# Rotary partners by VectorE's shuffle in place of products with a permutation matrix

## The chip, the cores and the metric

The kernel runs on one core of a Trainium2 chip. What counts is the device time of the whole kernel in microseconds (us), the median of several executions.

## What is computed

Two transformer blocks run one after the other over 512 tokens of width 1024, in fp32. The first mixes a gated recurrence over four heads with a windowed attention of eight query heads, then has a cross attention to a memory and a convolutional feed-forward part. The second runs a latent attention (MLA) and an attention to selected keys. Rotary embeddings stand in three places: on queries and keys of the windowed attention (the first 16 of 64 features of a head), and on the 32 rotary features of queries and of the one key of the latent attention.

```python
def rope(x, pos):
    half = x.shape[-1] // 2
    ...
    x1, x2 = x[..., :half], x[..., half:]
    return jnp.concatenate([x1 * cos - x2 * sin, x1 * sin + x2 * cos], axis=-1)
...
    qa = partial_rotary(q_a.reshape(B, S, ATT_Q_HEADS, ATT_HEAD_DIM), positions)
    ka = partial_rotary(k_a.reshape(B, S, ATT_KV_HEADS, ATT_HEAD_DIM), positions)
...
        q_nope, q_pe = q[..., :MLA_NOPE], rope(q[..., MLA_NOPE:], pos)
        k_pe = rope(k_rope[:, :, None, :], pos)[:, :, 0, :]
```

So each feature needs its partner, half a head away: x * cos + partner * sin, where the partner of the lower half carries a minus sign.

## The kernel before

Activations lie with features on the 128 partitions and the 512 tokens along the free axis. Every projection is three passes of TensorE (`three`, L579): weights and activations are split into a high and a low part. The weights come in slots of 128 x 1024 through a ring of four buffers; GpSimd splits each slot (`split`, L528: a tiny operation on `tick`, L533, then the high part, L534, then the low part, L536), two slots ahead at most, and starts on one when TensorE has finished the slot two before it.

All projections and transposes go through PSUM banks 0 and 1 in turn. `STREAM` (L80) lists them: an entry is a product with its number of slots, 0 where it takes no weights. Entry g uses bank g % 2, and `open_bank` (L574) waits until entry g - 2 has been read out (`freed`). The order of work on each engine is written out by hand, and engines meet only through semaphores.

A rotation took one product with a permutation matrix (`rotate` of TensorE, L640; the matrix `perm` swaps partners and carries the sign) into PSUM. VectorE then ran three operations (`rotate`, L1726): partners times sine (L1733), x times cosine in place (L1734), their sum (L1737). An fp32 product of 128x512 shows as two matmul records.

There are eight rotations. Those of the four query chunks `qa` and of the keys `ka` lie in the last head (h = 3) of the recurrence of the first block. TensorE runs products 0 and 1 in step `beside(3, 0)`, before `output(2)` (L781), and products 2 and 3 in `beside(3, 1)`, after the projection `k_a`; then come `tile_decays(3, 2)` (L733), `tile_scores(3, 1)` (L746), the projection `g_first`, `tile_decays(3, 3)`, and `tile_scores(3, 2)`, which needs `lev` of `select(3, 1)` (L1851). The keys' product stands between the transposes of `v_a` (L614) and the projection `g_rest`. VectorE rotates queries 0 and 1 before `tile(3, 1)` and queries 2 and 3 between `select(3, 0)` and `tile(3, 2)`; a `tile` is a run of 24 short products (L1842), a `select` one product with `level` (L1851) and one reduction (L1857). ScalarE makes the exponents of a tile (L1307). The keys are rotated after `select(3, 3)`. These five products had entries of their own in `STREAM`: `q_turn`, `q_turn2` and `k_turn`.

In the second block the key `kp` is rotated beside the gate `z_a`. The query chunks `qp` are rotated behind `ukv_k`: TensorE's two products stand before `ukv_v`, VectorE's part in the middle of the 16 rounds of `top_keys(1, r)` (L2239 to L2242). After that and two projections of `q_b` all three engines meet at a barrier (L555), before the latent attention.

Of the kernel before, what the change touches and what calls it, by code (L numbers as in the profile page):

```python
# [20 lines left out]
ALU = mybir.AluOpType  # L21
# [60 lines left out]
    ("q_turn", [0] * 2), ("k_a", [1]), ("q_turn2", [0] * 2), ("g_first", [1]), ("v_a", [1, 0]),  # L82
    ("k_turn", [0]), ("g_rest", [1] * 3),
# [25 lines left out]


def q_turn(c):

    return FIRST["q_turn"] + c if c < 2 else FIRST["q_turn2"] + c - 2
# [116 lines left out]
CONST_A = [("level", 8 * P), ("perm", P), ("band", 3 * P), ("spread", S), ("pick", P)]  # L230
CONST_D = [("perm", P), ("cos", S), ("sin", S), ("causal", S), ("onehot", TOEP), ("rep_k", P), ("rep_r", P), ("rep_p", P),
# [6 lines left out]
def build(nc, stream, xT, memT, pos, vecs, ident_d, const_r, const_a, const_d, sink_d, relb_d, gvec, x1_d, out_d):  # L238
    with ExitStack() as ctx:
# [185 lines left out]
        OUT_BANK = [(2, 3), (4, 5), (6, 1), (7, 0)]  # L425
# [51 lines left out]
        rot_done, rot_used, rotated = sem("rot_done"), sem("rot_used"), sem("rotated")  # L477
# [71 lines left out]
        def _(pe):  # L549
# [90 lines left out]
            def rotate(name, n, src, raw, perm, at=None, to=None):  # L640

                m = ROTATE[name] + n
                out_of_bank(pe, raw)
                if at is not None:
                    out = open_bank(at)
                else:
                    if n >= 2:
                        pe.wait_ge(rot_used, n - 1)
                    out = bank(4 + m % 2 if to is None else to)
                mm(out, perm, src, start=True, stop=True).then_inc(rot_done, 1)  # L650

# [35 lines left out]
            def recurrence(beside):  # L687
# [100 lines left out]
                for n in range(2):  # L788
                    pe.wait_ge(spreads, n + 1)
                    mm(bank(6 + n), c_a("pick", 0, P), wide[:, n, :], start=True, stop=True).then_inc(widened, 1)  # L790
# [151 lines left out]
            def head_beside(h, j):  # L942
                if h + 2 < HG_HEADS:
                    head_step(h + 2, j)
                elif h + 2 == HG_HEADS and j < 4:
                    project("q_a", j, 1, n_parts)
                elif h + 1 == HG_HEADS:
                    if j == 1:
                        project("k_a", 0, 1, n_parts)
                    if j < 2:  # L950
                        for c in (2 * j, 2 * j + 1):
                            rotate("first", c, qa[:, c, :], FIRST["q_a"] + c, c_a("perm", 0, P), q_turn(c))
                    elif j == 2:
                        project("v_a", 0, 1, n_parts)
                    elif j == 3:
                        turn_chunk("v_a", 0, 1, TURNED["v_a"])
                        rotate("first", 4, ka[:, :], FIRST["k_a"], c_a("perm", 0, P), FIRST["k_turn"])
                    elif j == 4:
                        project("g_rest", 0, 1, n_parts)
# [111 lines left out]
            rotate("second", 0, pk[:, :], FIRST["small"], c_d("rep_p", 0, P), to=6)  # L1071
# [36 lines left out]
            for c in range(2):  # L1108
                rotate("second", 1 + c, qp[:, c, :], FIRST["uq"] + 4 + c, c_d("perm", 0, P))

# [55 lines left out]
            def token_squares(x, start, stop):  # L1166
                for i in range(ST):
                    last = mm(bank(0)[:, i:i + 1], x[:, P * i:P * i + P], ones[:, 0:1],
                              start=start and i == 0, stop=stop and i == ST - 1)
                return last  # L1170
# [23 lines left out]
        def _(act):  # L1194
# [444 lines left out]
            A(ycol[:, :], bank(0)[:, :ST], ACT.Sqrt, scale=1.0 / D, bias=EPS).then_inc(std_made, 1)  # L1639
# [7 lines left out]
        def _(dve):  # L1647
# [78 lines left out]
            def rotate(name, n, x, cos, sin, at=None, to=None):  # L1726
                m = ROTATE[name] + n
                dve.wait_ge(rot_done, m + 1)
                if m:
                    dve.wait_ge(rotated, m)  # L1730
                partners, read = (bank(4 + m % 2 if to is None else to), rot_used) if at is None else (bank(at % 2), freed[at % 2])
                part = (sq if name == "second" else sgb)[:, m % 2, :]
                V.tensor_tensor(part, partners, sin, ALU.mult).then_inc(read, 1)  # L1733
                own(V.tensor_tensor(x, x, cos, ALU.mult))  # L1734
                if at is not None:
                    out_of_bank(dve, at)
                V.tensor_tensor(x, x, part, ALU.add).then_inc(rotated, 1)  # L1737
# [32 lines left out]
            def recurrence():  # L1770
# [117 lines left out]
                def turn_queries(c):  # L1888
                    rotate("first", c, qa[:, c, :], cosA[:, :], sinA[:, :], q_turn(c))

                for h in range(HG_HEADS):
                    more = h + 1 < HG_HEADS
                    if not more:
                        dve.wait_ge(tables, 2)
                        for c in (0, 1):
                            out_of_bank(dve, FIRST[f"head{2 + c}"] + 2)
                            turn_queries(c)
                    tile(h, 1)
                    select(h, 0)
                    if more:  # L1900
                        forget(h + 1)
                    else:
                        turn_queries(2)
                        turn_queries(3)
                    tile(h, 2)
                    select(h, 1)
                    tile(h, 3)
                    select(h, 2)
                    if more:
                        logs_low(h + 1)  # L1910
                    if h + 2 < HG_HEADS:
                        queries(h + 2)
                    select(h, 3)
                    if more:
                        start(h + 1)
                    else:
                        rotate("first", 4, ka[:, :], cosA[:, :], sinA[:, :], FIRST["k_turn"])
# [311 lines left out]
            rotate("second", 0, kp[:, :], c_d("cos", 0, S), c_d("sin", 0, S), to=6)  # L2229
# [47 lines left out]
            for c in range(2):  # L2277
                rotate("second", 1 + c, qp[:, c, :], c_d("cos", 0, S), c_d("sin", 0, S))
# [83 lines left out]
def rotary_partners(group, half):  # L2362

    m = np.zeros((P, P), np.float32)
    for g in range(0, P, group):
        for r in range(half):
            m[g + half + r, g + r] = -1.0
            m[g + r, g + half + r] = 1.0
    return m


def constants_a():
    c = level_constants()
    c["perm"] = rotary_partners(64, ROT_HALF)
# [6 lines left out]
    for g in (0, 64):  # L2381
        for r in range(2 * ROT_HALF):
            c["pick"][P // ROT_HALF * (r % ROT_HALF):P // ROT_HALF * (r % ROT_HALF + 1), g + r] = 1.0
    return [np.concatenate([np.asarray(c[n], np.float32) for n, _ in table], 1) for table in (CONST_R, CONST_A)]


def constants_d():
    c = {"perm": rotary_partners(32, 16)}
    freqs = np.float32(10000.0) ** (-np.arange(16, dtype=np.float32) / np.float32(16))
    angle = np.arange(S, dtype=np.float32)[None, :] * freqs[np.arange(P) % 16][:, None]  # L2390
    c["cos"], c["sin"] = np.cos(angle), np.sin(angle)
# [13 lines left out]
    c["rep_p"] = np.roll(c["perm"] * (np.arange(P)[:, None] < 32), 32, 0)[:, np.arange(P) % 32]  # L2405
# [123 lines left out]
```

## Time and profile before

| | |
|---|---|
| median of 3 runs | 1509.24 us (1509.18 to 1510.2) |
| the profiled execution | 1509.78 us, its span 1507.3 us |
| TensorE busy | 1449.6 us, 96% |
| VectorE busy | 942.1 us, 63% |
| GpSimd busy | 830.0 us, 55% |
| ScalarE busy | 453.8 us, 30% |
| TensorE in the chain that ended last | 81% |
| VectorE in that chain | 10% |

All times in the views are us from the start of the span. PE is TensorE, PEld its weight loads, PEldq its queue, DVE VectorE, ACT ScalarE, POOL GpSimd. A line of the chain tells what the end waited for at that moment; "issue" is time in which the engine waited for nothing that the profile shows. An idle time in brackets stands before the operation, with what ended it. `pair` is PSUM: two banks each. The granted clock (PEclk) is the share of full speed that TensorE was given: 1.00 is 2.4 GHz, 0.50 is 1.2 GHz.

### The profile page before, as it was taken

The page shows a single profiled execution, that of the slowest core. Times are in us where ns is not written, and L with a number is a line of the kernel's source. Part 1 is how long each engine was busy: PE and PEld are TensorE (multiplying, and loading weights), DVE is VectorE, ACT ScalarE, POOL GpSimd, SP SyncE. Part 2 cuts the span into 40 slices and gives each one's busy share as a digit, 9 for nine tenths or more (in the row PEclk, how much of TensorE's full clock was granted, in tenths as well). Part 3 has the DMA queues.
Part 4 walks back from the last instruction along what each step waited for, and adds up shares of the span by engine and source line. Part 5 has one row for each costly group of instructions (what it writes and reads, how often), then busy time and mean ns, then how long its engine had stood idle before and what let it go on. Part 6 is the DMA issues. An engine that isn't in the chain of part 4 may idle for free.

```text
span 1507.3 us, 19926 instructions
## 1 busy us (share of the span) xinstructions
PE 1449.6 (96%) x6948; PEld 1138.7 (76%) x6948; DVE 942.1 (63%) x1879; ACT 453.8 (30%) x887; POOL 830.0 (55%) x675
## 2 busy tenths in 40 slices
PE   4999999999999999999999999999999999999998
PEld 3777777676788788687888888887767777666887
DVE  6557797687238431567777764234767897686146
ACT  4555442366223111321010101112233334364112
POOL 3533323433566777266777777776655443444663
PEclk9999999999999999999999999999999999999999
DMA  5221111121333333132333333334225531322331
GB/s 205 72 70 43 43 42 43 56 66 54 106 97 98 112 112 103 51 98 84 98 98 98 98 97 99 98 112 134 84 73 153 105 89 46 113 78 88 117 96 67
DMA packets 37017, 135.59 MB, mean 90 GB/s; under 512 B 4296, under 2 KB 4552, under 8 KB 36296
## 3 DMA queue, kind: packets, MB, share of 16 engines
q1 hardware_dynamic: 33264, 121.13, 26.6%
q10 hardware_dynamic: 3672, 13.35, 3.4%
q8 instruction: 55, 0.90, 0.3%
q14 instruction: 26, 0.21, 0.0%
HBM read 127.64 MB, written 6.82 MB: 89 GB/s over the span
## 4 chain that ended last, share of the span: by engine, by line
PE 81%; DVE 10%; issue 4%; ACT 2%; POOL 1%; PEld 1%; DMA 0%; PEldq 0%; ACTq 0%; DVEq 0%; POOLq 0%
PE pair L581 23%; PE pair L583 22%; PE pair L582 22%; PE pair L851 3%; PE pair L879 3%; DVE X L1842 2%; PE pair L863 2%; PE pair L781 1%; DVE sums L1686 1%; POOL wL L536 1%; DVE lev L1851 1%; DVE rstd L1698 1%; DVE dx L1996 1%; POOL wH L534 1%; ACT E L1307 0%
## 5 line engine op out<-in xcount | busy, mean ns | idle before, releaser
L536 POOL TENSOR_TENSOR wL<-ring,wH 128x1024 fp32r<-128x1024 f32 x223 | 546.0, 2448 | 18.6
L581 PE MATMUL pair<-nH,wH 128*128 128x512 f32 x1064 | 426.9, 401 | 13.3 <-DVE nL L1677 8.2
L583 PE MATMUL pair<-nH,wL 128*128 128x512 f32 x1064 | 415.8, 391 | 0.0
L582 PE MATMUL pair<-nL,wH 128*128 128x512 f32 x1064 | 415.7, 391 | 0.0
L533 POOL TENSOR_TENSOR tick<-tick 128x1 f32<-128x1 f32 x223 | 55.5, 249 | 640.4 <-PE pair L583 631.1
L581 PEld LDWEIGHTS pair<-nH,wH 128*128 128x128 f32 x1064 | 200.1, 188 | 78.3 <-issue 27.5
L534 POOL TENSOR_SCALAR wH<-ring 128x1024 fp32r<-128x1024 f32 x223 | 237.4, 1065 | 0.0
L583 PEld LDWEIGHTS pair<-nH,wL 128*128 128x128 f32 x1064 | 200.3, 188 | 43.0
L582 PEld LDWEIGHTS pair<-nL,wH 128*128 128x128 f32 x1064 | 200.5, 188 | 40.4 <-issue 1.4
L1523 ACT ACTIVATE sgb<-cv 128x512 f32<-128x512 f32 x22 | 13.9, 634 | 209.6 <-DVE cv L2162 209.6
L1686 DVE TENSOR_TENSOR sums<-sums,sq 128x512 f32<-128x512 f32 (+1 forms) x37 | 60.1, 1623 | 18.4 <-ACT sq L1227 17.1
L581 PE MATMUL pair<-aH,wH 128*128 128x512 f32 x176 | 69.1, 393 | 0.0
L583 PE MATMUL pair<-aH,wL 128*128 128x512 f32 x176 | 68.6, 390 | 0.0
L582 PE MATMUL pair<-aL,wH 128*128 128x512 f32 x176 | 68.5, 389 | 0.0
L1842 DVE TENSOR_TENSOR X<-E,qT 128x64 f32<-128x64 f32 x192 | 35.1, 223 | 43.0 <-ACT E L1307 43.0
L2161 DVE SCALAR_TENSOR_TENSOR cv<-gpad,vec,cv 128x512 f32<-128x512 f32 x22 | 56.7, 2578 | 0.8
L1380 ACT ACTIVATE dx<-dx,stat 128x128 f32<-128x128 f32 (+3 forms) x64 | 36.0, 562 | 63.2 <-DVE stat L2002 63.0
L2188 DVE TENSOR_TENSOR hT<-pair,hT 128x512 f32<-128x512 f32 x8 | 5.5, 692 | 78.5 <-PE pair L583 78.5
L2014 DVE TENSOR_SCALAR dx<-dx,stat 128x128 f32<-128x128 f32 (+3 forms) x64 | 52.2, 816 | 2.3
L2158 DVE TENSOR_TENSOR gpad<-pair,rstd 128x512 f32<-128x512 f32 x22 | 15.2, 692 | 55.8 <-PE pair L583 55.8
L1307 ACT ACTIVATE E<-pair 128x768 f32<-128x768 f32 (+1 forms) x40 | 32.0, 852 | 42.4 <-PE pair L692 24.9
L1227 ACT ACTIVATE sq<-hT 128x512 f32<-128x512 f32 x28 | 17.7, 631 | 81.3 <-DVE hT L1743 48.3
(387 smaller groups left out, 2644.0 us busy)
## 6 DMA issues: line engine op xcount, KB each, us to landing
ring<-stream SPq DMA_DIRECT2D x223, 512.0 KB, 3.6
gvec<-gv ACTq DMA_DIRECT2D x1, 2560.0 KB
hT<-xT SPq DMA_DIRECT2D x4, 512.0 KB, 5.6
x_d<-hT ACTq DMA_DIRECT2D x1, 2048.0 KB, 7.2
toep<-gvec ACTq DMA_DIRECT2D x8, 256.0 KB, 3.5
hT<-x_d ACTq DMA_DIRECT2D x1, 2048.0 KB, 9.2
out<-yo SPq DMA_DIRECT2D x4, 512.0 KB, 3.6
cD<-const_d ACTq DMA_DIRECT2D x1, 1345.0 KB, 6.4
```

Source lines behind the costliest of these rows:

```text
L533: pool.tensor_tensor(tick[:, 1:2], tick[:, 0:1], tick[:, 0:1], ALU.add).then_inc(high_done, 1)
L534: pool.tensor_scalar(wH[:, r % SPL, :], ring[:, r, :], 1.0, 0.0, ALU.mult, ALU.add).then_inc(high_done, 1)
L536: pool.tensor_tensor(wL[:, r % SPL, :], ring[:, r, :], wH[:, r % SPL, :].bitcast(F32), ALU.subtract).then_inc(split_done, 1)
L581: mm(out, a[0], b[0], start=first, stop=False)
L582: mm(out, a[0], b[1], start=False, stop=False)
L583: return mm(out, a[1], b[0], start=False, stop=last)
L851: last = mm(out, *pairs[t], start=t == 0, stop=t == count - 1)
L879: last = mm(out[rows, qs], w, turned[:, j % 2, t, qs], start=n_t == 0, stop=n_t == len(kind["serves"]) - 1)
L1686: V.tensor_tensor(sums[:, :width], sums[:, :width], sq[:, a % 2, :width], ALU.add).then_inc(sq_added, 1)
L1842: last = V.tensor_tensor(two(X[:, m % 2, kind, xs])[:, half], factor(kind, d), two(src)[:, half], ALU.mult)
L2014: V.tensor_scalar(px, px, st[:, 5:6], None, ALU.mult).then_inc(a_prob, 1)
L2161: own(V.scalar_tensor_tensor(out=y, in0=x[:, 0:S], scalar=w[0], in1=y, op0=ALU.mult, op1=ALU.add))
```

## The change

Partners no longer come from TensorE. VectorE's `stream_shuffle` permutes partitions within each group of 32: it writes the partners of x to an SBUF buffer, and the product with the sine is then made in place in that buffer. The minus sign moves into the sine tables: the table of the first block is spread with `signed` in place of `pick`, and that of the second is made with its sign. The five entries without weights leave `STREAM`, so that everything after them changes between bank 0 and bank 1; the last products of the kernel follow with `last_bank`. The constants `perm` (twice) and `rep_p` go.

```diff
 STREAM = [
     ("head0", HEAD), ("head1", HEAD), ("head2", HEAD), ("head3", HEAD), ("q_a", [1] * 4),
-    ("q_turn", [0] * 2), ("k_a", [1]), ("q_turn2", [0] * 2), ("g_first", [1]), ("v_a", [1, 0]),
-    ("k_turn", [0]), ("g_rest", [1] * 3),
+    ("k_a", [1]), ("g_first", [1]), ("v_a", [1, 0]), ("g_rest", [1] * 3),
...
-CONST_A = [("level", 8 * P), ("perm", P), ("band", 3 * P), ("spread", S), ("pick", P)]
-CONST_D = [("perm", P), ("cos", S), ("sin", S), ("causal", S), ("onehot", TOEP), ("rep_k", P), ("rep_r", P), ("rep_p", P),
+CONST_A = [("level", 8 * P), ("signed", P), ("band", 3 * P), ("spread", S), ("pick", P)]
+CONST_D = [("cos", S), ("sin", S), ("causal", S), ("onehot", TOEP), ("rep_k", P), ("rep_r", P),
...
-        OUT_BANK = [(2, 3), (4, 5), (6, 1), (7, 0)]
+        last_bank = (FIRST["out2"] + DC - 1) % 2
+        OUT_BANK = [(2, 3), (4, 5), (6, last_bank), (7, 1 - last_bank)]
...
-            def rotate(name, n, src, raw, perm, at=None, to=None):
-
-                m = ROTATE[name] + n
-                out_of_bank(pe, raw)
-                if at is not None:
-                    out = open_bank(at)
-                else:
-                    if n >= 2:
-                        pe.wait_ge(rot_used, n - 1)
-                    out = bank(4 + m % 2 if to is None else to)
-                mm(out, perm, src, start=True, stop=True).then_inc(rot_done, 1)
...
-                    mm(bank(6 + n), c_a("pick", 0, P), wide[:, n, :], start=True, stop=True).then_inc(widened, 1)
+                    mm(bank(6 + n), c_a(("signed", "pick")[n], 0, P), wide[:, n, :], start=True, stop=True).then_inc(widened, 1)
...
-                    if j < 2:
-                        for c in (2 * j, 2 * j + 1):
-                            rotate("first", c, qa[:, c, :], FIRST["q_a"] + c, c_a("perm", 0, P), q_turn(c))
...
-                        rotate("first", 4, ka[:, :], FIRST["k_a"], c_a("perm", 0, P), FIRST["k_turn"])
...
-            rotate("second", 0, pk[:, :], FIRST["small"], c_d("rep_p", 0, P), to=6)
...
-            for c in range(2):
-                rotate("second", 1 + c, qp[:, c, :], FIRST["uq"] + 4 + c, c_d("perm", 0, P))
-
...
-            def rotate(name, n, x, cos, sin, at=None, to=None):
+            def rotate(name, n, x, cos, sin, half, group):
+
+
                 m = ROTATE[name] + n
-                dve.wait_ge(rot_done, m + 1)
+                swap = [i + half if i % group < half else i - half if i % group < 2 * half else i for i in range(32)]
                 if m:
                     dve.wait_ge(rotated, m)
-                partners, read = (bank(4 + m % 2 if to is None else to), rot_used) if at is None else (bank(at % 2), freed[at % 2])
                 part = (sq if name == "second" else sgb)[:, m % 2, :]
-                V.tensor_tensor(part, partners, sin, ALU.mult).then_inc(read, 1)
+                V.stream_shuffle(part, x, swap).then_inc(swapped, 1)
+                dve.wait_ge(swapped, m + 1)
+                V.tensor_tensor(part, part, sin, ALU.mult).then_inc(part_made, 1)
                 own(V.tensor_tensor(x, x, cos, ALU.mult))
-                if at is not None:
-                    out_of_bank(dve, at)
+                dve.wait_ge(part_made, m + 1)
                 V.tensor_tensor(x, x, part, ALU.add).then_inc(rotated, 1)
...
                 def turn_queries(c):
-                    rotate("first", c, qa[:, c, :], cosA[:, :], sinA[:, :], q_turn(c))
+                    out_of_bank(dve, FIRST["q_a"] + c)
+                    rotate("first", c, qa[:, c, :], cosA[:, :], sinA[:, :], ROT_HALF, 32)
...
-                        rotate("first", 4, ka[:, :], cosA[:, :], sinA[:, :], FIRST["k_turn"])
+                        out_of_bank(dve, FIRST["k_a"])
+                        rotate("first", 4, ka[:, :], cosA[:, :], sinA[:, :], ROT_HALF, 32)
...
-            rotate("second", 0, kp[:, :], c_d("cos", 0, S), c_d("sin", 0, S), to=6)
+            rotate("second", 0, kp[:, :], c_d("cos", 0, S), c_d("sin", 0, S), 16, 32)
...
-                rotate("second", 1 + c, qp[:, c, :], c_d("cos", 0, S), c_d("sin", 0, S))
+                out_of_bank(dve, FIRST["uq"] + 4 + c)
+                rotate("second", 1 + c, qp[:, c, :], c_d("cos", 0, S), c_d("sin", 0, S), 16, 32)
...
+    c["signed"] = c["pick"] * np.where(np.arange(P) % 64 < ROT_HALF, -1.0, 1.0)
...
-    c["cos"], c["sin"] = np.cos(angle), np.sin(angle)
+    c["cos"] = np.cos(angle)
+    c["sin"] = np.sin(angle) * np.where(np.arange(P) % 32 < 16, -1.0, 1.0)[:, None]
```

## Rows read from the trace of the kernel before

**Rows 1.** The page: busy time by engine, and the shares of the chain that ended last
```profile
PE 1449.6 (96%) x6948; PEld 1138.7 (76%) x6948; DVE 942.1 (63%) x1879; ACT 453.8 (30%) x887; POOL 830.0 (55%) x675
...
PE 81%; DVE 10%; issue 4%; ACT 2%; POOL 1%; PEld 1%; DMA 0%; PEldq 0%; ACTq 0%; DVEq 0%; POOLq 0%
```

**Rows 2.** The chain in order of time, first block: start us, us, what
```profile
215.23 3.09 PE pair L650 x4
218.32 3.43 PE pair L781 x8
...
240.03 1.76 DVE X L1842 x13
...
244.64 1.58 PE pair L746 x12
...
255.34 0.86 PE pair L650 x2
...
264.33 5.25 PE pair L781 x8
```

**Rows 3.** Timeline of TensorE: start us, us, engine line op out<-in, count [idle before <-releaser]
```profile
213.83 0.45 PE L733 MATMUL pair<-cR,lftH 64*128 64x384 f32 x2 [2.03 <-ACT E L1307]
...
1142.09 1.88 PE L650 MATMUL pair<-qp,cD 128*128 128x512 f32 x4
```

**Rows 4.** Three stretches: us, busy by engine, granted clock (PEclk), DMA share, GB/s
```profile
215.00:218.30 3.30, 3.30 (x7) 1.50 (x6) 3.30 (x14) 1.51 (x2) 0.00 (x0) 0.61 0.00 0
264.30:269.70 5.40, 5.27 (x9) 1.89 (x8) 3.16 (x13) 0.28 (x2) 1.24 (x1) 0.68 0.32 97
1097.00:1104.00 7.00, 7.00 (x29) 4.78 (x26) 3.56 (x6) 1.96 (x5) 1.34 (x1) 1.00 0.25 75
```

**Rows 5.** Timeline of ScalarE, first block
```profile
215.28 1.51 ACT L1307 ACTIVATE E<-pair 128x768 f32<-128x768 f32 x2 [1.01 <-PE pair L733]
```

**Rows 6.** Timeline of VectorE, first block
```profile
169.70 2.96 DVE L1811 TENSOR_TENSOR E<-E,kk 128x256 f32<-128x256 f32 x2
...
228.79 0.36 DVE L1842 TENSOR_TENSOR X<-E,qT 128x64 f32<-128x64 f32 x2 [3.86 <-ACT E L1307]
...
235.77 1.49 DVE L1734 TENSOR_TENSOR qa<-qa,cosA 128x512 f32<-128x512 f32 x1
```

**Rows 7.** Timeline of VectorE: the operations nearest to a shuffle
```profile
216.79 0.29 DVE L1794 COPY xk<-kk 128x256 f32<-128x256 f32 x1
...
233.30 1.96 DVE L1857 TENSOR_REDUCE Sg<-lev 128x128 f32<-128x1024 f32 x1
```

**Rows 8.** Timeline of GpSimd, first block
```profile
169.32 2.72 POOL L536 TENSOR_TENSOR wL<-ring,wH 128x1024 fp32r<-128x1024 f32 x1
174.55 2.48 POOL L533 TENSOR_TENSOR tick<-tick 128x1 f32<-128x1 f32 x1 [2.51 <-PE pair L583]
...
234.34 2.38 POOL L536 TENSOR_TENSOR wL<-ring,wH 128x1024 fp32r<-128x1024 f32 x1
243.28 0.19 POOL L533 TENSOR_TENSOR tick<-tick 128x1 f32<-128x1 f32 x1 [6.56 <-PE pair L583]
```

**Rows 9.** The chain in order of time, second block
```profile
1094.61 1.99 issue
...
1098.95 0.86 PE pair L650 x2
...
1156.29 4.11 PEldq L555
```

**Rows 10.** Timeline of VectorE, second block
```profile
1105.96 0.69 DVE L1721 TENSOR_TENSOR za<-pair,sgb 128x512 f32<-128x512 f32 x1 [3.02 <-ACT sgb L1272]
...
1149.41 0.42 DVE L2239 MAX8 best<-selm 128x8 f32<-128x256 f32 x1
...
1155.30 1.09 DVE L2242 TENSOR_SCALAR selm<-selm 128x256 f32<-128x256 f32 x1
```

**Rows 11.** Timeline of GpSimd, second block
```profile
1149.70 1.05 POOL L534 TENSOR_SCALAR wH<-ring 128x1024 fp32r<-128x1024 f32 x1
```

More of the change, by code:

```diff
@@ L108, in running @@
     return at, n
-def q_turn(c):
-    return FIRST["q_turn"] + c if c < 2 else FIRST["q_turn2"] + c - 2
 def g_r(c):
@@ L476, in build @@
         y_left, y_right = sem("y_left"), sem("y_right")
-        rot_done, rot_used, rotated = sem("rot_done"), sem("rot_used"), sem("rotated")
+        swapped, part_made, rotated = sem("swapped"), sem("part_made"), sem("rotated")
         f_made, lf_made, lf_turned, lh_made, lft_made, zero_one = (
@@ L1167, in token_squares @@
                 for i in range(ST):
-                    last = mm(bank(0)[:, i:i + 1], x[:, P * i:P * i + P], ones[:, 0:1],
+                    last = mm(bank(1 - last_bank)[:, i:i + 1], x[:, P * i:P * i + P], ones[:, 0:1],
                               start=start and i == 0, stop=stop and i == ST - 1)
@@ L1638, in _ @@
             act.wait_ge(sum_done, NORMS.index("out") + 1)
-            A(ycol[:, :], bank(0)[:, :ST], ACT.Sqrt, scale=1.0 / D, bias=EPS).then_inc(std_made, 1)
+            A(ycol[:, :], bank(1 - last_bank)[:, :ST], ACT.Sqrt, scale=1.0 / D, bias=EPS).then_inc(std_made, 1)
             act.wait_ge(r_made, NORMS.index("out") + 1)
@@ L2359, in level_constants @@
     return out
[L2362 to L2369, printed above, removed]
 def constants_a():
     c = level_constants()
-    c["perm"] = rotary_partners(64, ROT_HALF)
     q, k = np.arange(P)[:, None], np.arange(3 * P)[None, :] - P
@@ L2383, in constants_a @@
             c["pick"][P // ROT_HALF * (r % ROT_HALF):P // ROT_HALF * (r % ROT_HALF + 1), g + r] = 1.0
+    c["signed"] = c["pick"] * np.where(np.arange(P) % 64 < ROT_HALF, -1.0, 1.0)
     return [np.concatenate([np.asarray(c[n], np.float32) for n, _ in table], 1) for table in (CONST_R, CONST_A)]
 def constants_d():
-    c = {"perm": rotary_partners(32, 16)}
+    c = {}
     freqs = np.float32(10000.0) ** (-np.arange(16, dtype=np.float32) / np.float32(16))
     angle = np.arange(S, dtype=np.float32)[None, :] * freqs[np.arange(P) % 16][:, None]
-    c["cos"], c["sin"] = np.cos(angle), np.sin(angle)
+    c["cos"] = np.cos(angle)
+    c["sin"] = np.sin(angle) * np.where(np.arange(P) % 32 < 16, -1.0, 1.0)[:, None]
     q, k = np.arange(P)[:, None], np.arange(S)[None, :] - (S - P)
@@ L2404, in constants_d @@
     c["rep_r"] = np.arange(P)[:, None] == 32 + np.arange(P)[None, :] % 32
-    c["rep_p"] = np.roll(c["perm"] * (np.arange(P)[:, None] < 32), 32, 0)[:, np.arange(P) % 32]
     c["parity"] = np.arange(P)[:, None] // 32 % 2 == np.arange(2)[None, :]
```

## The prediction

> **What bounds the kernel now.** I read the page's busy times first, then the shares of the chain that ended last. TensorE is busy 96% of the span and holds 81% of the chain; VectorE is busy 63% and holds 10% of it [rows 1]. So a product taken from TensorE is worth its length only where TensorE holds the chain, and a VectorE instruction added costs nothing only where it does not. The next view is therefore the chain in order of time around the eight products removed. Four fp32 products with `perm` stand for the queries of the first block, one for its keys, three for the second block; one product is two matmul records and takes 0.86 us on the chain, as the one at 255.34 [rows 2]. Around the first four the chain passes from TensorE to VectorE and back [rows 2]; that is where the argument is hard. Third come the timelines of VectorE, ScalarE and GpSimd there, and the granted clock.
>
> **First block, queries 0 and 1.** Their products hold the chain for 3.09 us, four records at 215.23 [rows 2], against 1.88 us for four such records at 1142.09, and TensorE had stood idle 2.03 us before L733 at 213.83 [rows 3]: the granted clock was 0.61 from 215.00 to 218.30, a mix of 1.2 and 2.4 GHz [rows 4]. With them gone, `output` (L781) still waits for ScalarE's exponents, which end at 215.28 + 1.51 = 216.79 [rows 5]. It starts 1.5 us earlier than 218.32 [rows 2], but runs its first microsecond in the slow clock; I take 1.0 us earlier (1.5 if the clock is back at once; 0.8 us later than now if the slow clock also covers all of L781, which cost 5.25 - 3.43 = 1.8 us once [rows 2]). After its two rotations VectorE idles 3.86 us before the run of products at 228.79 [rows 6]. Two shuffles fit in there.
>
> **What a shuffle costs.** The trace has none. The nearest rows are a copy of 256 elements at 0.29 us, so 0.6 for 512, and a reduction of 1024 elements at 1.96 us, so 1.0 for 512 [rows 7]. Nearest is the copy, which likewise has one input and one output; I take 0.7 with the wait behind it, and keep 0.6 and 1.0 as ends. The Trainium skill, "VectorE: DVE Perf Modes", section "The perf-mode tier table", gives a shuffle about 2400 ns for 2048 elements; scaled, an estimate of 0.6, which would make each pair of shuffles 0.2 us cheaper. No run here shows it.
>
> **Queries 2 and 3** lie between `select(3,0)` and `tile(3,2)`, where VectorE holds the chain from 228.79 to 244.64 [rows 2, 6]. Two shuffles add 1.4 us. A second effect comes with them: the product with the sine read PSUM and SBUF and now reads SBUF twice. In this trace VectorE products with two SBUF inputs wait while GpSimd splits weights: L1811 needed 2.96 us for a pair while the split ran 169.32 + 2.72 = 172.04 [rows 6, 8]. The cosine product at 235.77 took 1.49 us because the split at 234.34 ended at 236.72 [rows 6, 8]. After the change the sine product meets that wait instead, so it is not paid twice; the shuffle, with one input, runs beside the split, and that recovers about 0.1. Net: 1.0 earlier, 1.4 more, 0.1 back: TensorE gets `lev` at 244.95 in place of 244.64, 0.3 later (between 0.5 earlier and 2.2 later by the ends above).
>
> **The hole this leaves on TensorE.** Its part of the same stage loses another two products (1.9 us) and so finishes `g_first` at about 243.28 - 1.0 - 1.9 = 240.4, which is where GpSimd's next split would start (L533, now at 243.28) [rows 8]. With 0.9 us of decays behind it TensorE then idles from 241.3 to 244.95, 3.6 us; now it works through nearly all of this. The clock fell once after an idle stretch of 2.03 us, and again with L781 after narrow products (0.68 granted from 264.30 to 269.70) [rows 4]. I expect one more stretch at 1.2 GHz, right where TensorE takes over the chain. The price of a full one is the 1.8 us above; part of it may fall into the hole: 1.4 (ends 0 and 1.8).
>
> **Keys.** Product at 255.34, 0.86 us, TensorE before and after it on the chain [rows 2]: 0.86 gained. VectorE's shuffle is hidden there: nothing of the chain returns to VectorE before L781. First block: +0.3 + 1.4 - 0.86 = +0.8 us.
>
> **Second block, key.** 0.86 us at 1098.95, TensorE on the chain on both sides [rows 9]: gained. VectorE idles 3.02 us before the next gate at 1105.96 [rows 10], which hides 0.7.
>
> **Second block, queries.** Four records at 1142.09, two products, 1.72 us at 0.86 each [rows 3]. The next meeting of all engines is the barrier, which TensorE releases last, at 1156.29 + 4.11 = 1160.40 [rows 9]. Without these and the key's product it gets there at 1160.40 - 2.58 = 1157.82. VectorE is done at 1155.30 + 1.09 = 1156.39 [rows 10]. For it: 0.86 earlier, two shuffles 1.4 later, and the split. The split now at 1149.70 (L534, and L536 for another 2.4) moves 2.58 forward to 1147.1 and ends about 1150.7 [rows 8, 11]. Today the rotations are over at 1149.41 [rows 10] and miss it; then it lies across the whole second rotation, one of whose SBUF products waits up to 2.4 us. VectorE would end at 1156.39 - 0.86 + 1.4 + 2.4 = 1159.3, or 0.8 sooner if L2242 no longer meets a split. I take 1159.0: VectorE becomes the last at the barrier and 1.2 us of the gain is lost (ends 0 and 1.7, and 0.6 more for a shuffle of 1.0). Second block: -0.86 - 1.72 + 1.2 = -1.4 us.
>
> **At nothing:** the sign moved into tables (same copies and products as before, one constant for another of equal size), a 131 KB smaller constant load, the waits of `k_a` and `g_first` on older banks, and the swap of banks 0 and 1 for all that follows, since five entries leave the list; both banks are used alike. What hides the older waits is TensorE's own work on the entries between; without it they would cost less than a product.
>
> **Sum.** +0.8 - 1.4 = -0.6 us (0.55 unrounded). The profiled execution took 1509.78 with a span of 1507.3, 0.54 above the median of 1509.24. Against its own time the sum gives 1509.2; against the median 1508.7, my forecast. About 0.2%, 3.0 us, is what a measurement of this kernel can tell from no change.
>
> **Rivals.**
> Everything is covered (22%): the clock stays at 2.4 GHz behind the hole, the barrier stays TensorE's. Then 0.3 - 0.86 - 0.86 - 1.72 = -3.1, with the early gain at 1.5 in full -3.6; time 1505.8 in the middle. For it: after 1.99 us of idle time at 1094.61 the granted clock stayed at 1.00 [rows 4, 9]. Against: the hole is nearly twice that.
> The split meets the run of 24 short products (18%), slower than before. VectorE would begin `tile(3,2)` at 240.03 + 0.3 = 240.35 [rows 2], GpSimd its split at 240.4, together within the error of both. If GpSimd's L534 is in first, the run is held for 1.05 + 2.4 us, 3.2 of it lost, and TensorE waits: -0.6 + 3.2 = +2.6, 1511.9. It decides from a start of the run later than about 240.55 (a shuffle over 0.8, or an earlier split). Against it: at 174.55 GpSimd asked inside such a run and waited 2.48 us, to the run's end [rows 8]. The Trainium skill, "SBUF — State Buffer", section "Who interferes with whom", says the engine that issues first gets the shared ports for the whole instruction and the other blocks. By that rule the split would get in between two short products, which is this rival; the row at 174.55 shows it kept out of the run, and the rule agrees with the 2.96 us.
> The shuffle is dear, or takes part in the quarrel with GpSimd (10%): at 1.0 us each, 0.6 more in each place where VectorE decides, +0.6 in all: 1509.9.
> Forecast as worked out: 50%.
>
> **How the numbers follow.** Faster by over 0.2% needs the first rival, three parts in four of it, and little of the forecast: 0.20. Slower by over 0.2% needs the second, somewhat over half of it, and tails of the third and the forecast: 0.14. The rest, 0.66. The range runs from about the first rival's middle, 1505.6, to near the second's, 1511.6, which leaves half of each out, about one in five.
>
> **What would show it.** In the profile after: L781 near 217.3; VectorE's shuffles 0.6 to 0.7; a sine product stretched at about 235; TensorE idle over 3 us before the `lev` that it takes at about 244.9, with a granted clock under 1 behind; GpSimd's L533 at about 240.4 lasting 2 us or more (forecast) or VectorE's X products stretched (second rival); 0.86 less at the keys; at the barrier TensorE waiting for VectorE rather than the other way. The forecast is wrong if the clock stays up in the hole, if the barrier is still TensorE's, or if the split holds the run.

## The result, and the profile after

The changed kernel takes 1517.08 us (1515.12 to 1519.82), the kernel before beside it 1509.18 (1506.80 to 1510.20): a ratio of 1.0051, 95% interval 1.0039 to 1.0062, so slower by some 8 us. The forecast was 1508.7 with a range to 1511.6. The profiled execution took 1519.82 us with a span of 1517.8, 10.5 more than the span of before; all shifts in this section are between these two traces.

The page first: span, busy times and shares of the chain. Line numbers have moved: L764 is `output` (L781 before), L729 the scores over X (L746), L1709 to L1714 the rotation (L1733 to L1737), L1819 the run X (L1842), L1828 `lev` (L1851), L576 to L578 the split products (L581 to L583), L528, L529 and L531 GpSimd's tick, `wH` and `wL` (L533, L534, L536).

```profile
span 1517.8 us, 19905 instructions
PE 1449.2 (95%) x6932; PEld 1141.3 (75%) x6932; DVE 953.8 (63%) x1895; ACT 454.1 (30%) x887; POOL 829.7 (55%) x675
PE 81%; DVE 11%; issue 3%; ACT 2%; POOL 1%; DMA 0%; ACTq 0%; DVEq 0%; POOLq 0%
```

Sixteen matmul records are gone, and yet TensorE is as long busy as before (1449.6 in [rows 1]): what remains ran longer. VectorE has 11.7 us more. Next, the chain in order of time in the first block: start us, us, what.

```profile
215.61 1.52 ACT E L1282 x2
217.27 5.19 PE pair L764 x8
...
235.92 0.76 DVE sgb L1709 x2
236.70 1.24 DVE sgb L1711
...
242.10 4.80 DVE X L1819 x13
246.90 1.57 DVE X L1819 x11
248.47 1.15 DVE lev L1828
249.75 2.90 PE pair L729 x12
```

`output` starts 1.05 us earlier than at 218.32 [rows 2], as forecast, but takes 5.19 us in place of 3.43. The run X of tile 2, 3.3 us before (1.76 and 1.57 in that trace's chain), takes 6.37. Why, the timelines of GpSimd and VectorE show:

```profile
242.06 0.19 POOL L528 TENSOR_TENSOR tick<-tick 128x1 f32<-128x1 f32 x1 [4.67 <-PE pair L578]
242.21 1.04 POOL L529 TENSOR_SCALAR wH<-ring 128x1024 fp32r<-128x1024 f32 x1
243.34 2.34 POOL L531 TENSOR_TENSOR wL<-ring,wH 128x1024 fp32r<-128x1024 f32 x1
```

```profile
241.49 0.69 DVE L1714 TENSOR_TENSOR qa<-qa,sgb 128x512 f32<-128x512 f32 x1
242.10 1.23 DVE L1819 TENSOR_TENSOR X<-E,qT 128x64 f32<-128x64 f32 x2
243.25 2.51 DVE L1819 TENSOR_TENSOR X<-E,kk 128x64 f32<-128x64 f32 x2
245.69 0.35 DVE L1819 TENSOR_TENSOR X<-E,qT 128x64 f32<-128x64 f32 x2
```

Two of these short products need 0.35 us. The first pair ends with GpSimd's `wH` (243.25), the second with its `wL` (245.68), and only then does the run go on. This is the mechanism of the prediction's second rival; its price of 3.2 us measured 3.0.

TensorE's side, with the idle time before each, and the granted clock of the stretches behind (us, busy by engine, PEclk, DMA share, GB/s). 0.50 is the lower of the two levels, 1.2 GHz, throughout.

```profile
249.75 2.90 PE L729 MATMUL pair<-X 128*128 128x128 f32 x12 [6.95 <-DVE lev L1828]
1168.36 0.49 PE L834 MATMUL pair<-kn,qn 64*128 64x128 f32 x4 [1.60 <-DVEq L1628]
```

```profile
217.27:222.46 5.19, 5.19 (x10) 2.41 (x11) 5.16 (x30) 0.00 (x0) 0.00 (x0) 0.71 0.00 0
249.75:254.50 4.75, 4.75 (x19) 4.54 (x20) 4.75 (x24) 0.00 (x0) 0.00 (x0) 0.50 0.00 0
1170.32:1176.00 5.68, 5.68 (x13) 4.45 (x14) 2.86 (x10) 2.59 (x6) 0.22 (x1) 0.50 0.62 97
```

The second block's end on VectorE and GpSimd:

```profile
1156.29 0.74 DVE L1709 STREAM_SHUFFLE sq<-qp 128x512 f32<-128x512 f32 x1
1157.07 0.70 DVE L1711 TENSOR_TENSOR sq<-sq,cD 128x512 f32<-128x512 f32 x1
1157.69 2.88 DVE L1712 TENSOR_TENSOR qp<-qp,cD 128x512 f32<-128x512 f32 x1
1160.60 0.69 DVE L1714 TENSOR_TENSOR qp<-qp,sq 128x512 f32<-128x512 f32 x1
...
1167.11 1.14 DVE L2221 TENSOR_SCALAR selm<-selm 128x256 f32<-128x256 f32 x1
```

```profile
1157.31 2.71 POOL L531 TENSOR_TENSOR wL<-ring,wH 128x1024 fp32r<-128x1024 f32 x1
...
1166.90 0.19 POOL L528 TENSOR_TENSOR tick<-tick 128x1 f32<-128x1 f32 x1 [1.76 <-PE pair L578]
1167.06 1.04 POOL L529 TENSOR_SCALAR wH<-ring 128x1024 fp32r<-128x1024 f32 x1
```

The cosine product, 0.68 us alone, waits for `wL`; the last instruction ahead of the barrier meets `wH` (it took 1.09 in [rows 10] too, but there 4 us before TensorE arrived). TensorE stands 1.60 us.

Laying the same instructions of both traces beside each other gives this account, in us of delay against before, each entry the growth of the shift from one instruction to the next:

| Where | Adds | Shift then |
|---|---|---|
| `output` and what leads to it, slow clock | +0.70 | 0.70 |
| rotations of queries 2 and 3: started 0.05 later, 6.18 in place of 4.86 | +1.37 | 2.07 |
| run X of tile 2 held by the split | +3.03 | 5.10 |
| slow clock behind TensorE's 6.9 us without work | +2.25 | 7.34 |
| the keys' product gone | -0.94 | 6.40 |
| drift to 1080 us | +0.15 | 6.55 |
| a sums product of 1081.8 held by `wH`, where before it came first; slow clock behind | +0.90, +1.61 | 9.06 |
| second block's key product gone | -0.86 | 8.20 |
| its queries' two products gone | -1.76 | 6.44 |
| VectorE late at the barrier | +1.48 | 7.92 |
| slow clock behind the barrier | +2.68 | 10.60 |

The profiled execution lies 2.7 us above the median. That is about one entry of clock, and the likeliest reading is that not every execution has all of them; this is argued, since only one execution has a trace.

### The profile page after: what moved, and what is told of

Read it like the earlier page. It is cut to its first block, busy times and chain, and to the rows that moved or that the text cites. A ratio compares the mean times of both kernels' runs of the same rounds, so it can differ in the third digit from the quotient of the medians.

```text
span 1517.8 us, 19905 instructions
## 1 busy us (share of the span) xinstructions
PE 1449.2 (95%) x6932; PEld 1141.3 (75%) x6932; DVE 953.8 (63%) x1895; ACT 454.1 (30%) x887; POOL 829.7 (55%) x675
## 4 chain that ended last, share of the span: by engine, by line
PE 81%; DVE 11%; issue 3%; ACT 2%; POOL 1%; DMA 0%; ACTq 0%; DVEq 0%; POOLq 0%
PE pair L576 23%; PE pair L578 22%; PE pair L577 22%; PE pair L834 3%; PE pair L862 3%; DVE X L1819 2%; PE pair L846 2%; PE pair L764 1%; DVE sums L1661 1%; POOL wL L531 1%; DVE lev L1828 1%; DVE rstd L1673 1%; DVE dx L1975 1%; DVE selm L2232 1%; ACT E L1282 1%
## 5 line engine op out<-in xcount | busy, mean ns | idle before, releaser
L531 POOL TENSOR_TENSOR wL<-ring,wH 128x1024 fp32r<-128x1024 f32 x223 | 545.9, 2448 | 18.6
L576 PE MATMUL pair<-nH,wH 128*128 128x512 f32 x1064 | 429.3, 403 | 13.4 <-DVE nL L1652 8.2
L578 PE MATMUL pair<-nH,wL 128*128 128x512 f32 x1064 | 417.2, 392 | 0.0
L528 POOL TENSOR_TENSOR tick<-tick 128x1 f32<-128x1 f32 x223 | 55.7, 250 | 651.3 <-PE pair L578 641.9
L576 PEld LDWEIGHTS pair<-nH,wH 128*128 128x128 f32 x1064 | 201.3, 189 | 78.2 <-issue 27.5
L529 POOL TENSOR_SCALAR wH<-ring 128x1024 fp32r<-128x1024 f32 x223 | 236.8, 1062 | 0.0
L578 PEld LDWEIGHTS pair<-nH,wL 128*128 128x128 f32 x1064 | 201.2, 189 | 43.3
L576 PE MATMUL pair<-aH,wH 128*128 128x512 f32 x176 | 69.0, 392 | 0.0
L578 PE MATMUL pair<-aH,wL 128*128 128x512 f32 x176 | 68.5, 389 | 0.0
L1819 DVE TENSOR_TENSOR X<-E,qT 128x64 f32<-128x64 f32 x192 | 36.0, 230 | 42.1 <-ACT E L1282 42.1
```

The lines of the kernel that those rows point to most:

```text
L528: pool.tensor_tensor(tick[:, 1:2], tick[:, 0:1], tick[:, 0:1], ALU.add).then_inc(high_done, 1)
L529: pool.tensor_scalar(wH[:, r % SPL, :], ring[:, r, :], 1.0, 0.0, ALU.mult, ALU.add).then_inc(high_done, 1)
L531: pool.tensor_tensor(wL[:, r % SPL, :], ring[:, r, :], wH[:, r % SPL, :].bitcast(F32), ALU.subtract).then_inc(split_done, 1)
L576: mm(out, a[0], b[0], start=first, stop=False)
L578: return mm(out, a[1], b[0], start=False, stop=last)
L1819: last = V.tensor_tensor(two(X[:, m % 2, kind, xs])[:, half], factor(kind, d), two(src)[:, half], ALU.mult)
```

## Experiments

They go from "which half" to "which wait" to "which order of work avoids it". In each, "before" is the kernel before, run beside it: 1509.45 us for `one_moved` and the three `early3` kernels, 1509.4 for `first_moved` and the two `spaced` ones, 1509.36 for the other eight.

### One block at a time

In `first_only` the second block keeps its three products, in `second_only` the first keeps its five. The edits are the change's own hunks, for one block only.

> First block by shuffle, second block by products as in the kernel before. The theory: the loss arises in the first block, where VectorE's rotations of queries 2 and 3 end so late that GpSimd's split gets in ahead of tile 2's short products X (3.0 us of stall) and TensorE, idle for some 7 us, gets the slow clock afterwards. It expects about 1516 us (1514.5 to 1517.5), X run of tile 2 at 242 us with rows of 1.2 and 2.5 us in it, and the end of the first block some 6 us late. Rival: the loss is spread over both blocks, 1512 us.

> First block by products as before, second block by shuffle. The theory: three products less on TensorE (-2.6 us), VectorE late at the barrier by 1.5 us, and perhaps one stretch of slow clock behind that wait (up to 2.7 us): 1508.0 to 1510.8, most likely 1509.5. Rival (the second block carries a half of the loss): 1513 us.

Measured: `first_only` 1517.08, ratio 1.0053 (1.0039 to 1.0067); `second_only` 1508.37, ratio 0.9997 (0.9988 to 1.0006). The whole loss is the first block's. Its trace repeats the one above: TensorE idle 6.95 us before tile 2's `lev`. The second block's trace has TensorE waiting 1.60 us at the barrier, and no gain that can be measured.

### The products kept for nothing

`first_filled`: VectorE shuffles in the first block, and TensorE still makes the five products (with another matrix of the same size), which nobody reads.

```
 # VectorE, first block (condensed)
+own(V.stream_shuffle(part, x, swap)); partners = part
 V.tensor_tensor(part, partners, sin, ALU.mult).then_inc(read, 1)   # read frees the product's bank
```

> The kernel before, but in the first block VectorE takes the partners from its shuffle, and TensorE still makes its five products, which nobody reads; second block as before. The theory (VectorE is late, whatever TensorE does in the meantime): the X run of tile 2 is still met by the split if it starts at 242 us, and the time is 1513 to 1516. Rival (the hole on TensorE, which the products filled, costs the time through the clock): the products fill it, and the time is 1509 to 1511.

Measured: 1513.42, ratio 1.0026 (1.0016 to 1.0037), 3.7 us below `first_only` with the same work on VectorE. The number is the theory's, its reason is not. VectorE (first fence) and GpSimd (second):

```profile
243.13 0.35 DVE L1845 TENSOR_TENSOR X<-E,qT 128x64 f32<-128x64 f32 x2
...
246.38 1.22 DVE L1854 TENSOR_TENSOR lev<-pair,cA 128x1024 f32<-128x1024 f32 x1
```

```profile
244.95 1.57 POOL L533 TENSOR_TENSOR tick<-tick 128x1 f32<-128x1 f32 x1 [6.54 <-PE pair L583]
```

The run starts 1 us later than in the changed kernel and isn't held: the split is released by TensorE's last product out of that slot of weights, and the rotary products ahead of it on TensorE put that off to 244.95, into the run, where the tick waits for the run's end. So the products removed had paced the split: with them it asks 1.8 us after the run's start, without them 0.04 us before it. The same rotations with a split released at 242.06 (changed kernel) or 242.67 (`first_only`) cost 3 us more. What is left, 4.1 us by the medians, shows in this trace as the longer pair of rotations (1.4) and as slow clock ahead of them (1.6) and behind TensorE's 2.06 us without work (1.6).

### Shorter rotations, and products gone alone

Both leave the partners out, and with them the shuffle, `no_shuffle23` for queries 2 and 3, `no_shuffle_all` for all eight. The sine product reads x itself:

```
-V.stream_shuffle(part, x, swap)
-V.tensor_tensor(part, part, sin, ALU.mult)
+V.tensor_tensor(part, x, sin, ALU.mult)
```

> The kernel after without the shuffle in the rotations of queries 2 and 3 (the partners are left out there: the sine product reads the query itself), so that each is one instruction of 0.75 us shorter. The theory (a race at 242.1 us between GpSimd's split and tile 2's X run, lost by 0.04 us): the run now starts at 240.6, before the split's tick at 242.1, which has to wait for its end; the run takes 3.3 us in place of 6.4, TensorE's idle stretch falls from 6.9 to about 2.4 us, and the time is that of after less 1.5, less 3.0, less up to 1.4 of clock: 1511.0 to 1513.0. Rival (the time follows the length of VectorE's work alone): 1517.1 - 1.5 = 1515.6.

> The kernel after with all eight shuffles left out (the partners are left out: the sine product reads the row block itself): VectorE does as much as in the kernel before, TensorE has eight products less. It prices the removal of the products alone. Theory: X run before the split as above, second block 2.6 us shorter on TensorE and VectorE late at the barrier by no more than 0.3: 1508 to 1510.5. Rival (holes on TensorE without its products cost the time by the clock): 1513 or more.

Measured: 1513.99, ratio 1.0026 (1.0017 to 1.0035), and 1514.11, ratio 1.0027 (1.0016 to 1.0037). VectorE and GpSimd in `no_shuffle23`:

```profile
236.33 2.03 DVE L1710 TENSOR_TENSOR sgb<-qa,sinA 128x512 f32<-128x512 f32 x1
...
241.73 0.36 DVE L1822 TENSOR_TENSOR X<-E,qT 128x64 f32<-128x64 f32 x2
```

```profile
242.49 2.62 POOL L528 TENSOR_TENSOR tick<-tick 128x1 f32<-128x1 f32 x1 [4.68 <-PE pair L578]
```

The race is shown: a run that starts 0.76 us ahead of the tick keeps GpSimd out to its end, 2.62 us; TensorE's idle stretch is 3.09 us in place of 6.95. But the two shuffles left out (1.5 us) shortened the pair of rotations by only 0.78: the sine product then stands in the split itself. 3.1 us came back, less than expected, and one part of that miss is this. The other shows in `no_shuffle_all`, where I missed by 3.6 us and the rival's number held. In its profiled execution the shift against before is -0.3 us at 264 and +0.1 at the barrier, so neither block loses by work; it comes behind the barrier, 2.8 us of it, in a stretch of slow clock after TensorE's 1.60 us. Taking TensorE's products away, with VectorE no slower than before, makes holes of 1.70, 3.09 and 1.60 us. In this execution the clock fell behind the first and the last of them and stayed at 1.00 behind the second. The execution, 1512.22, lies 1.9 us below the median, and no trace shows what the others had besides.

### The rotations put elsewhere

`moved` turns query 2 ahead of tile 1's run (VectorE idled 2.89 us there) and query 3 after the selection of tile 2 (3.36 us). `one_moved` moves only query 3. `first_moved` is `moved` with the second block's products kept.

```
 # last head, condensed
 for c in (0, 1): ... turn_queries(c)
+turn_queries(2)                  # moved, first_moved
 tile(h, 1); select(h, 0)
-turn_queries(2); turn_queries(3) # one_moved keeps query 2 here
 tile(h, 2); select(h, 1); tile(h, 3); select(h, 2)
+turn_queries(3)
 ...
```

> The kernel after, with query 2's rotation put ahead of tile 1's X run, where VectorE idles 2.9 us, and query 3's behind tile 3's X run and the selection of tile 2, where it idles 3.4 us. The theory (late rotations and the split in the X run): tile 2's X run starts at about 236 us without a stall, TensorE's idle stretch of 6.9 us goes to below 1 us, and the time is 1508.0 to 1510.5. Rival (removing TensorE's work makes the holes, wherever VectorE puts its own): 1513 to 1516.

> The kernel after with query 3's rotation alone put behind tile 3's X run and the selection of tile 2; query 2's stays where it was. The theory (a race for the ports at 242 us): tile 2's X run starts at about 239.5 and is nearly over when the split comes, so that one rotation of some 3.5 us put off saves more than its own length: tile 2's lev at 243 us in place of 248.4, and the time is 1509.5 to 1511.5. Rival (each rotation costs its own length, both the same): halfway between after and the kernel with both moved, 1513.5.

> First block by shuffle with query 2's rotation ahead of tile 1 and query 3's behind tile 3's X run and the selection of tile 2, second block by products as before. The theory: the first block ends 1.8 to 2.0 us earlier than before, as in the trace of 'moved', the second is that of the kernel before: 1507.0 to 1508.5. Rival (the 2 us in that trace were a matter of where the slow clock fell): 1509.0 to 1510.0.

Measured: `moved` 1509.87, ratio 1.0001 (0.9992 to 1.0011); `one_moved` 1510.07, ratio 1.0003 (0.9991 to 1.0015); `first_moved` 1509.55, ratio 0.9999 (0.9990 to 1.0008). The order alone gives back the 7 us. In `one_moved` VectorE reads

```profile
239.57 0.36 DVE L1819 TENSOR_TENSOR X<-E,qT 128x64 f32<-128x64 f32 x2
...
242.82 1.22 DVE L1828 TENSOR_TENSOR lev<-pair,cA 128x1024 f32<-128x1024 f32 x1
```

The second row is 5.6 us before the 248.38 of the changed kernel, for one rotation of some 3.5 us taken from the path: the run was 2.9 us old when the split's tick came at 242.47. The median falls as far as with both moved. That is a race decided, not a length: the rival's 1513.5 is out.

`first_moved` missed, and the rival's number held. Its trace is 1.6 us ahead of before at 264 and 0.3 behind at 1100: behind the 1.99 us without work that TensorE has at 1095 in both kernels, the clock falls in this one and did not in the profile of before. That is not a trait of this kernel: of the fifteen traces with this wait twelve fell to 0.68 behind it, `before_early3` (products in both blocks) among them, and three stayed at 1.00, those of before, of the changed kernel and of `second_only`. In `moved` that stretch reads (second row; the first is behind the barrier)

```profile
1159.14:1164.00 4.86, 3.62 (x21) 2.91 (x22) 3.60 (x15) 3.25 (x7) 2.17 (x1) 1.00 0.51 81
1094.73:1100.00 5.27, 5.27 (x15) 3.20 (x16) 1.20 (x3) 2.46 (x5) 1.72 (x1) 0.68 0.36 99
```

### The barrier of the second block

`moved`, `one_moved`, `second_only` and `no_shuffle_all` all wait 1.60 us there, though VectorE's load differs. First I took VectorE's length for the cause and shifted work. In the `early` kernels the final norm's products go ahead of the second reciprocal (all eight, or three in `early3`), and rounds of the top-keys search take their place:

```
 # condensed
 norm("q_lat", ...)
+for c in range(3): final_normed(c)        # range(8) in the first form
 inverse("c_kv")
```

> The kernel before, with the eight products of the final norm on VectorE put ahead of the reciprocal of the second block, where VectorE idles some 5 us, and three rounds of the top-keys search taken forward into the places they leave. Control for the next run: VectorE isn't late at the barrier there, so nothing changes: 1509.2, 1508.3 to 1510.0. Rival (this shift is worth something by itself): below 1507.5.

> The kernel 'moved' with the same shift in the second block. The theory: TensorE's wait of 1.60 us for VectorE at the barrier goes, and with it the slow clock that some runs have behind it: 1505.5 to 1508.3, most likely 1507.0. Rival (another releaser is as late at the barrier, or the wait costs nothing): 1509.0 to 1510.

> The kernel 'moved' with three of the final norm's products (2.1 us) put where VectorE idles 3.7 us before the second reciprocal, clear of the split that comes 1 us later, and two rounds of top keys taken forward into their place. The theory: VectorE's last instruction before the barrier starts before the split's tick and isn't stretched from 0.29 to 1.14 us, TensorE's wait of 1.60 us at the barrier falls to below 0.7, the slow clock behind it goes, and the time is 1505.5 to 1508.0. Rival (the three products meet the split as the eight did, and put off the second reciprocal): above 1510, with the wait ahead of the transposes of the new keys above 2.5 us in place of 1.99.

> The kernel 'second_only' (first block by products, second by shuffle) with the same shift of three products. The theory: -2.6 us for the products without the wait at the barrier: 1506.0 to 1507.5. Rival as above: above 1509.

> The kernel before with the same shift of three products, as a control: VectorE is 3.8 us early at the barrier there, so both theories that blame VectorE's lateness expect nothing: 1509.2 (1508.5 to 1510.0). Rival: the shift is worth something or costs something by itself, over 1.5 us either way.

Measured: `before_early` 1515.47, ratio 1.0038 (1.0024 to 1.0052; the profiled execution was its fastest, 1511.50), `moved_early` 1513.34, ratio 1.0020 (1.0010 to 1.0030). VectorE and TensorE in the first:

```profile
1083.26 8.31 DVE L2225 SCALAR_TENSOR_TENSOR hT<-hT,vec,rstd 128x512 f32<-128x512 f32 x8
```

```profile
1097.74 1.09 PE L1067 MATMUL pair<-ident,pk 128*128 128x128 f32 x4 [6.47 <-issue]
```

Eight products of 5.5 us took 8.31, since a split lay across them; the reciprocal came after them, and TensorE passed on 4.5 us later than with its usual 1.99. So "issue" in front of those transposes is a wait for VectorE's `c_kv` in all the kernels, and the idle time ahead of the reciprocal was no cover for 5.5 us. With three of them: `moved_early3` 1509.73, ratio 1.0000 (0.9991 to 1.0008), `second_early3` 1509.94, 1.0001 (0.9992 to 1.0011), `before_early3` 1509.95, 1.0000 (0.9991 to 1.0008). They do no harm, and no good: the wait is 1.60 us as ever. It is the split's length and not VectorE's: in the changed kernel TensorE stops at 1166.76, the tick starts at 1166.90, VectorE's last instruction 0.2 us later, `wH` ends at 1168.10 and that instruction with it. VectorE in `moved_early3`:

```profile
1143.71 2.92 DVE L1711 TENSOR_TENSOR sq<-sq,cD 128x512 f32<-128x512 f32 x1
...
1149.49 2.88 DVE L1712 TENSOR_TENSOR qp<-qp,cD 128x512 f32<-128x512 f32 x1
...
1158.91 1.14 DVE L2224 TENSOR_SCALAR selm<-selm 128x256 f32<-128x256 f32 x1
```

The 2 us saved ahead of the rotations were handed to the split: the first sine product, 0.95 in `moved`, now takes 2.92. The splits come at TensorE's pace, and VectorE's products with two SBUF inputs fall in step with them. The remedy is then not less work but another order. `moved_spaced` and `second_spaced` put the second rotation four rounds of top keys later, where no split runs; those rounds (MAX8, MATCH_REPLACE8) are not stretched by splits in these traces.

```
 for c in range(2):
     rotate("second", 1 + c, qp[:, c, :], ...)
-for r in range(10, 16): top_keys(1, r)
+    for r in ((10, 11, 12, 13), (14, 15))[c]: top_keys(1, r)
```

> The kernel 'moved' with four rounds of top keys put between the two rotations of the second block's queries, so that the second rotation starts some 4 us later and its four instructions run between two splits. The theory: its cosine product takes 0.7 us and not 2.9, VectorE reaches its last instruction 2.2 us earlier, before the split's tick, which takes that one from 1.14 to 0.29 us; TensorE's 1.60 us at the barrier falls to below 0.7, and the time is 1506.0 to 1508.5. Rival (the hold only moves to another product, as with 'moved_early3'): the wait stays 1.60 and the time 1509.0 to 1510.5.

> The kernel 'second_only' with the same order of rounds and rotations. The theory: 1506.0 to 1508.0, the wait at the barrier below 0.7. Rival: wait of 1.60 us and 1508.0 to 1509.5.

Measured: `moved_spaced` 1506.47 (1504.72 to 1507.42), ratio 0.9979 (0.9970 to 0.9988); `second_spaced` 1506.86, ratio 0.9985 (0.9976 to 0.9994). VectorE, then TensorE and GpSimd, in `moved_spaced`:

```profile
1152.55 0.69 DVE L1711 TENSOR_TENSOR sq<-sq,cD 128x512 f32<-128x512 f32 x1
1153.15 0.69 DVE L1712 TENSOR_TENSOR qp<-qp,cD 128x512 f32<-128x512 f32 x1
1153.88 1.57 DVE L1714 TENSOR_TENSOR qp<-qp,sq 128x512 f32<-128x512 f32 x1
...
1157.32 0.53 DVE L2221 TENSOR_SCALAR selm<-selm 128x256 f32<-128x256 f32 x1
```

```profile
1158.65 0.49 PE L834 MATMUL pair<-kn,qn 64*128 64x128 f32 x4
```

```profile
1158.69 0.19 POOL L528 TENSOR_TENSOR tick<-tick 128x1 f32<-128x1 f32 x1 [0.99 <-PE pair L578]
```

The cosine product is back at 0.69, the add still catches 0.9 us of a split, and VectorE is through at 1157.85, ahead of the next tick and of TensorE, which passes the barrier without a wait. Against `moved` only the order of six rounds differs: 3.4 us, twice the wait itself. The same order against `second_only` gave 1.5 us, so how much of the 3.4 is clock isn't shown. Eight of the eleven times of `moved` lie above 1509.4, none of `moved_spaced` above 1507.5. In the traces the clock fell behind the barrier in the changed kernel, `no_shuffle_all`, `one_moved`, `moved_early`, `moved_early3` and `second_early3`, all of which wait there (0.69 us in `moved_early`, 1.60 in the rest), not in three others that wait 1.60 us, and in none where TensorE doesn't wait, `moved_spaced` and `second_spaced` among them. `moved_spaced` is the change with its gain, 0.2% faster than the kernel before and by the medians 0.7% faster than the change as made. Nearly all of that gain is the second block's: `second_spaced`, which keeps the first block's five products, is 2.5 us faster than before, and shuffling in the first block as well adds 0.4 us, less than these runs can tell. No run puts the new order of rounds into the kernel before; TensorE doesn't wait there, so nothing is expected of it.

## Why the prediction was wrong

**Bounds and queries 0 and 1.** `output` did start 1.05 us earlier. It then took 5.19 us: granted clock 0.71. I had written nearly this end down (0.8 later than now) and chosen the other. The shift of +0.70 in place of -1.0 is the first mis-sized term, 1.7 us, and it decided more than its size. The later end for `lev` was also summed too small: 0.8 late and two shuffles of 1.0 us give 2.7, not 2.2. Without the stall the trace has 2.07.

**The shuffle** was right: 0.73 to 0.75 us, 0.76 with its mask, against the 0.7 taken. The pair of rotations grew by 1.32, forecast 1.3, with the sine product stretched at 236.70 as described. The Trainium skill's figure, "VectorE: DVE Perf Modes", section "The perf-mode tier table", scaled, gave an estimate of 0.6; the trace measures a quarter more. That it ran beside the split held too, but one input is not what decides: TENSOR_SCALAR, with one tensor input, took 1.14 us beside the split and 0.29 alone.

**The split and the run** is the step that failed. I put the run's start at 240.35 and the split's at 240.4 and gave the quarrel 18%. Measured: 242.10 and 242.06. Both moved by the same 1.7 us of slow clock, the gap stayed within 0.1 us, and GpSimd was first. With two times that close it should have been an even chance; I had entered one outcome of a race in the sum as if it were a term, and thought the split needed a lead of 0.15 us (240.55 against 240.4) where 0.04 was enough. The coin is the forecaster's and not the chip's: `first_only` has GpSimd first again, by 0.02 us, and all ten times of the two kernels are above 1515. The row at 174.55 [rows 8], which I held against this rival, shows only what happens when VectorE is first; so does `no_shuffle23`. Its price was right, 3.0 for 3.2. The Trainium skill's rule, "SBUF — State Buffer", section "Who interferes with whom", is that whoever issues first has the shared ports for the whole instruction and the other blocks. The changed kernel's trace agrees on GpSimd's side: VectorE's short products pass only between `wH` and `wL`. On VectorE's side the trace of `no_shuffle23` shows more than one instruction held: GpSimd waited 2.62 us through a run of products of which a pair takes 0.35.

**The hole and its clock.** Forecast 3.6 us of idle time and 1.4 for the clock; measured 6.95 and 2.25. Of the hole's extra length the stall is 3.0.

**Keys** 0.94 for 0.86.

**Second block.** Key 0.86 for 0.86, queries 1.76 for 1.72, VectorE late by 1.48 for 1.2, by one SBUF product of the second rotation as forecast, and by the last instruction, which met the next split. Missing from the sum was the clock behind that wait, 2.7 us in the profiled execution: I had priced slow clock behind one hole and not behind the next. `second_only` puts the block at -0.4 us (-1.8 to +0.9) where I had -1.4; `second_spaced`, 1.5 us below `second_only`, shows what the wait and the clock had cost there. Together the terms named so far, 1.7, 3.0, 0.9 for the clock behind the hole, 0.3 and 2.7, make 8.6 of the 11.1 us between the forecast and the profiled execution; the other 2.5 are the next paragraph's.

**At nothing.** The constants, the signs and the swap of banks: no trace shows a cost. The sums product at 1081.8, held by `wH` in the changed kernel and not before, lies outside the changed code. With the clock behind it, it cost 2.5 us. In the traces of all fifteen kernels run afterwards TensorE's wait there is 1.03 to 1.05 us, as in that of before, so that entry belongs to the profiled execution rather than to the change.

What stays open: which holes the clock answers in a given execution. `no_shuffle_all` is at 1514 without a loss of work in its trace, and `first_moved` lost 1.6 us behind a hole that the kernel before has as well. The traces show the clock falling there, not what decides it. The kernel before varies too: of its last 27 times 5 lie at 1507.5 to 1507.8, 14 at 1509.2 to 1509.7 and 7 at 1510.7 to 1511.1. One stretch of slow clock more or less would make such steps; with one trace this is argued and not shown.

## What to carry to other kernels

Where VectorE's products and GpSimd's split hold each other up, a term "this one starts 0.05 us before that one" is a coin to the forecaster, and both sides of it belong in the forecast, with the stall and TensorE's slow clock behind it. Removing work from TensorE also moves forward whatever its progress releases; look up what that is and what it will meet. An addition to VectorE is best put where it idles or between operations that the split doesn't hold, and spacing can be worth more than less work.

## What the runs showed of the hardware

- A shuffle of 128x512 fp32 within 32 partitions took 0.72 to 0.76 us, and was not stretched by a split that ran beside it (0.74 at 1156.29, 0.75 at 235.92); the sine product behind it was.
- Of VectorE's instructions in these traces the products with two SBUF inputs (0.68 us at 128x512, up to 2.92) and the TENSOR_SCALAR of 128x256 (0.29 to 1.14 us) wait for a split. MAX8 and MATCH_REPLACE8 don't (0.42 to 0.43 and 0.41 us at 128x256 either way), nor does the product `lev` with one input in PSUM (1.21 to 1.23 us either way).
- A run of 24 short products kept GpSimd's tick of 0.19 us waiting 2.62 us, to its end.
- After 0.7 to 7 us without work on TensorE the granted clock of what followed was often down to 0.50 to 0.74, and where the cost was read above it was 1.6 to 2.8 us. Behind the same 1.99 us at 1095 it stayed at 1.00 in three traces, that of before among them, and fell to 0.68 in twelve. At `output`, with 1.70 us without work in front, it was 0.50 to 0.62 over the first 4 us in all ten traces that lack the products of queries 0 and 1.
